# A two-block fp32 transformer kernel: joined seams, the compressed branch by token, and the convolution's layer norm in columns

## The chip, the cores and the metric

The kernel runs on one core of a Trainium2 chip. The metric is device time in microseconds (us) from start to end of one execution. Inputs and outputs are fp32 in HBM. The core has TensorE (PE in the rows), VectorE (DVE), ScalarE (ACT), GpSimd (POOL), SyncE (SP), and DMA queues that SyncE and ScalarE feed.

## What is computed

512 tokens of width 1024 pass a first block (latent attention beside a depthwise convolution, a gated FFN, a gated per-layer embedding) and then a second block of two layers: a short convolution mixer and an MLP, then a sparse attention and an MLP. The parts that the change touches, from the reference:

```python
def hybrid_mixer(xn, ...):                       # first block
    ...
    attn = causal_mla_attention(q_nope, q_rope, k_nope, k_rope, v)
    c = causal_depthwise_conv(a * jax.nn.sigmoid(gate), conv_w, conv_b)
    c = jax.nn.silu(layer_norm(c, conv_ln_g, conv_ln_b))
    return jnp.concatenate([attn, c], axis=-1) @ w_o

def first_block(...):
        ...
        h = h + rms_norm(ffn, g_ffn_post[i])
        e = rms_norm(p[i] @ w_ple_proj[i], g_ple[i])
        h = h + jax.nn.sigmoid(h @ w_ple_gate[i]) * e

def nsa_attention(...):                          # second block, layer 2
        logit_c = jnp.einsum('bqghd,bngd->bqghn', qt, k_cmp) + bias_c[None]
        p_c = jax.nn.softmax(logit_c, axis=-1) * has_any[None, :, None, None, None]
        o_c = jnp.einsum('bqghn,bngd->bqghd', p_c, v_cmp)
        ...
        o = gt[..., 0:1] * o_c + gt[..., 1:2] * o_s + gt[..., 2:3] * o_w
```

With 512 tokens the selection keeps every block, so selected and window branches are two softmaxes over the same causal range. The compressed keys are 31 blocks of 32 tokens, each passed through a two-layer MLP with SiLU (`phi`). `gt` are sigmoid gates, 16 heads by 3. `bias_c` and the other biases come from a table of relative positions.

## The kernel before

**Layout and precision.** Activations lie as channels in partitions and tokens in columns: `h[:, c, :]` is chunk c of 8, 128 channels by 512 tokens. An fp32 product is made of rounded halves: x = XH + XL, w = WH + WL, and three matmuls (WH·XH, WH·XL, WL·XH, `three`, lines 399 to 403). HH and HL are a second pair of such halves.

**Weights.** There are 301 units of 128x1024, loaded by SyncE in one fixed order into a ring of four slots, `raw`. ScalarE makes WH (`upper`, line 891), GpSimd makes WL = raw − WH (line 370), and a projection of TensorE waits for `wlo` and then runs 24 matmuls of 512 columns to a unit (`project`, `by_token`). `upper(b.u + k)` casts on ScalarE all units up to k ahead of the one in use, each when its slot has been released (`used`).

**Order.** Nothing is scheduled: each engine has its program written out by hand, in which it runs strictly in order, and semaphores join them. PSUM has eight banks of 128x512: 0 to 3 take output tiles in turn (`tile_done`, `tile_free`), 4 to 7 serve norms, tables and attention. VectorE or ScalarE evicts a tile, and VectorE makes the low half of every activation.

**Norms.** Squares are made by ScalarE (line 913) and added up by VectorE (line 1424); `total` sums over partitions on TensorE (line 492), ScalarE takes the root (line 920), VectorE the reciprocal (line 1430), `spread` brings it back as a full tile (line 501).

**Start.** VectorE computes the rotary angles (`rope_table`, line 1491) between the input projection's tiles 0 to 1 and 2 to 3, whose eviction is `channels(2)`, line 1517.

**First attention.** After the convolution (line 513, 128x128 matmuls) come the low-rank expansions: four units for the queries, two for keys and values. Then the layer norm's sum over channels (`ln_total`, line 521: fp32 matmuls with a stationary matrix of ones), then four pairs of heads: scores (534, 539), logits on VectorE, exponentials on ScalarE (1049), transposes (550), copies (1057), values (568), whose result ScalarE evicts (1063). The layer norm's second sum (521 again), its root, reciprocal, products, SiLU (1088) and splits stand inside pairs 1 to 3. Then the output projection `w_o`.

**FFN's end.** TensorE sums the squares, `spread`; VectorE makes h + norm chunk by chunk (1698, 1700) and its low half (1793); ScalarE makes the high half. The gate projection (8 units, two rounds of 4) starts on the first chunks. After each round ScalarE takes the sigmoid (1212), VectorE multiplies and adds, and `lower_chunk` (1795, 1799) prepares the first MLP's input, the short convolution mixer's.

**Tables.** In the second block's mixer, after its group j = 1, TensorE makes 16x1680 biases (line 581, four matmuls), VectorE copies them (1829), and ScalarE issues two DMAs that repeat them in HBM (`ftab`, `tab`, lines 1239, 1241); they are read back as bias strips in the attention.

**Compressed branch.** `phi` is two projections of 96 matmuls of 160 columns each; a second layer (746, 751); query projection (8 units in two rounds of 4); gates by token (96 matmuls of 48 columns); logits by key (24 matmuls of 512 columns, KCH stationary) into banks 0 to 3; VectorE copies them and adds the bias (2022, 2026); 16 transposes (774) bring them to tokens; VectorE takes maximum, difference (2038, 2041), later sum, reciprocal and product (2047 to 2058); 16 transposes (786) bring them back.

**Second attention.** 16 pairs, each of two heads in one of the two branches: scores (805), logits (2068), exponentials (1364), normalising (2085), transposes (817), copies of them (1370, `pair_copy`), values (831, 840), and after every second pair the eviction `pair_out` (1376, 1378). Then the output projection: two projections of four units, and the last MLP.

Of the kernel before, what the change touches and what calls it, by code (L numbers as in the profile page):

```python
# [8 lines left out]
S, D, P = 512, 1024, 128  # L9
# [4 lines left out]
PH = 4  # L14
# [40 lines left out]
n1_done t1_done p1_g0 p1_rest v1_done v1_out at_hi at_lo ln_sum ln_xc ln_sq ln_var ln_std ln_inv ln_xn ln_act cv_hi cv_lo warm y_out y_tmp e_g ffn_t ffn_g ffn_gelu ffn_u hid_s hid_hi  # L55
hid_lo r_ok v_ok y_ok cu_t tab_done tab_out tab_st bc_in col_ok kv_ok kr_ok kr_pad kr_hi kr_lo silu_ok
cmp_done kc_hi kc_lo vc_ok gate_s gate_ok c_lg c_mx lt_ok c_exp c_sum c_inv c_mul c_tr c_pt krep_hi krep_lo
# [69 lines left out]
def build(nc, io):  # L127
# [3 lines left out]
    with ExitStack() as ctx:  # L131
# [75 lines left out]
        ohs, relb, tabs, bcs = cut(12304, 1680), cut(13984, H2), cut(5636, 1680), cut(9728, GR, S)  # L207
# [12 lines left out]
        qst, L, PCT, LT = cut(6144, TT, S), cut(12288, TT, S), cut(6144, GR, S), cut(6144, GR, S)  # L220
# [6 lines left out]
        NMX, SUM, INV, COL, RC = 16, 32, 48, 80, 84  # L227
# [34 lines left out]
        LOGITS2 = (4, 6, 8)  # L262
        NP1 = H1 // 2
# [53 lines left out]
        def _(sp):  # L317
# [27 lines left out]
            for hd in range(H2):  # L345
                if hd < 4:
                    sp.wait_ge(sems["kr_lo"], 2)
                    if hd == 3:
                        sp.wait_ge(sems["lt_ok"], GR)
# [45 lines left out]
        def _(pe):  # L395
# [121 lines left out]
            def ln_total(x, ready, done):  # L517

                for c in range(4):
                    ready(c)  # L520
                    last = nc.tensor.matmul(ps[:, 6, :], ones[:, :], x[:, c, :], start=c == 0, stop=c == 3)
                last.then_inc(sems[done], 1)
# [20 lines left out]
            def mla_transposes(n, r):  # L543
                j = 2 * n + r
                pe.wait_ge(sems["n1_done"], 4 * (j + 1))
# [27 lines left out]
            def tables():  # L573

                pe.wait_ge(sems["onehot_in"], 16)
                pe.wait_ge(sems["relb_in"], 16)
                for k in range(0, 1680, S):
                    if k >= 2 * S:
                        pe.wait_ge(*m["tab_out"].upto(k // S - 1))
                    w = min(S, 1680 - k)  # L580
                    nc.tensor.matmul(ps[0:H2, 4 + k // S % 2, 0:w], relb[0:33, 0:H2], ohs[0:33, k:k + w],
                                     start=True, stop=True).then_inc(*m["tab_done"].tick())
                m["tab_out"].next(4)
# [1677 lines left out]
```

## Time and profile before

| what | value |
|---|---|
| median of 3 runs | 2014.56 us (2013.85 to 2014.84) |
| profiled execution, whole | 2016.62 us |
| its span, first to last instruction | 2014.6 us |
| mean granted TensorE clock | 0.965 |
| TensorE busy | 1914.2 us, 95% |
| VectorE, ScalarE, GpSimd busy | 992.1, 763.7, 756.5 us |
| DMA | 177.53 MB, 88 GB/s over the span |

Durations are read from the one profiled execution. "Busy" of TensorE includes time at a lower clock. The granted clock is a share of 2.4 GHz: 0.50 is the level of 1.2 GHz. A profile names each instruction by engine, source line and operation, and for an engine's idle time the instruction that ended it.

### The profile page before, as it was taken

The numbers are of one execution on the slowest core, as the hardware profiler recorded it, in microseconds if no ns is written. First come the engines' busy times: TensorE is split into PE (matmuls) and PEld (weight loads), VectorE is DVE, ScalarE is ACT, GpSimd is POOL, SyncE is SP. The second block draws the span as 40 slices with busy tenths as digits, with TensorE's granted clock in tenths as the row PEclk, the third lists the DMA queues.
The fourth block names the chain that finished last, engine by engine and source line by source line (L and its number), as shares of the span: only waits on it lengthen the run. The fifth ranks groups of instructions, "written<-read, shape, count | busy, mean of one in ns | idle before, by whom it ended". The sixth has DMA issues, their size and how long they took to land.

```text
span 2014.6 us, 25069 instructions
## 1 busy us (share of the span) xinstructions
PE 1914.2 (95%) x9252; PEld 1556.7 (77%) x9252; DVE 992.1 (49%) x1635; ACT 763.7 (38%) x1297; POOL 756.5 (38%) x319
## 2 busy tenths in 40 slices
PE   7899898999999799999999999999788899999997
PEld 6786586888888677888888888888655588888886
DVE  6656368543445644235433345631677635334444
ACT  6676544222223341233222223322288733222221
POOL 4412133534443332444554444534100035444442
PEclk9999899999999899999999999988799999999999
DMA  5202122332333233973333322333010123332321
GB/s 183 69 37 63 31 84 65 116 92 86 112 96 92 63 91 82 168 178 107 90 108 95 101 85 88 111 94 110 6 33 27 48 76 103 101 96 83 100 89 62
DMA packets 52236, 177.53 MB, mean 88 GB/s; under 512 B 5527, under 2 KB 5911, under 8 KB 52152
## 3 DMA queue, kind: packets, MB, share of 16 engines
q1 hardware_dynamic: 47952, 166.22, 26.7%
q10 hardware_dynamic: 4200, 10.15, 3.4%
q8 instruction: 57, 0.93, 0.2%
q14 instruction: 27, 0.22, 0.0%
HBM read 166.88 MB, written 9.47 MB: 88 GB/s over the span
## 4 chain that ended last, share of the span: by engine, by line
PE 81%; issue 9%; DVE 6%; POOL 2%; ACT 2%; DMA 0%; ACTq 0%; DVEq 0%; POOLq 0%
PE ps L401 25%; PE ps L402 25%; PE ps L403 25%; POOL WL L370 2%; PE ps L513 2%; DVE arena L2085 1%; DVE arena L2068 1%; PE ps L840 1%; PE ps L817 1%; PE ps L805 1%; ACT arena L1364 1%; DVE arena L1491 0%; PE ps L831 0%; ACT arena L1370 0%; DMA ident<-in_ident 0%
## 5 line engine op out<-in xcount | busy, mean ns | idle before, releaser
L370 POOL TENSOR_TENSOR WL<-raw,WH 128x1024 fp32r<-128x1024 f32 x295 | 736.0, 2509 | 1202.2 <-ACT WH L891 1202.1
L401 PE MATMUL ps<-XH,WH 128*128 128x512 f32 (+1 forms) x1280 | 503.1, 393 | 33.0 <-DMA ident<-in_ident 10.6
L891 ACT ACTIVATE WH<-raw 128x1024 fp32r<-128x1024 f32 x295 | 303.8, 1053 | 538.8 <-PE ps L403 481.5
L402 PE MATMUL ps<-XL,WH 128*128 128x512 f32 (+1 forms) x1280 | 500.9, 391 | 0.0
L403 PE MATMUL ps<-XH,WL 128*128 128x512 f32 (+1 forms) x1280 | 500.4, 391 | 0.0
L401 PE MATMUL ps<-HH,WH 128*128 128x512 f32 x1072 | 420.4, 392 | 3.7 <-DVE HL L1799 3.7
L402 PE MATMUL ps<-HL,WH 128*128 128x512 f32 x1072 | 419.0, 391 | 0.0
L403 PE MATMUL ps<-HH,WL 128*128 128x512 f32 x1072 | 418.8, 391 | 0.0
L401 PEld LDWEIGHTS ps<-XH,WH 128*128 128x128 f32 x1280 | 248.2, 194 | 85.4 <-issue 29.8
L403 PEld LDWEIGHTS ps<-XH,WL 128*128 128x128 f32 x1280 | 248.2, 194 | 49.1
L402 PEld LDWEIGHTS ps<-XL,WH 128*128 128x128 f32 x1280 | 248.2, 194 | 47.7
L401 PEld LDWEIGHTS ps<-HH,WH 128*128 128x128 f32 x1072 | 202.5, 189 | 46.2 <-issue 4.5
L403 PEld LDWEIGHTS ps<-HH,WL 128*128 128x128 f32 x1072 | 202.3, 189 | 42.5
L402 PEld LDWEIGHTS ps<-HL,WH 128*128 128x128 f32 x1072 | 202.3, 189 | 41.7
L1912 DVE TENSOR_TENSOR h<-h,ps 128x512 f32<-128x512 f32 x112 | 75.6, 684 | 161.0 <-PE ps L403 161.0
L1895 DVE SCALAR_TENSOR_TENSOR arena<-ps,rstd 128x512 f32<-128x512 f32 x64 | 44.0, 691 | 195.7 <-PE ps L403 188.7
L1447 DVE TENSOR_TENSOR XL<-arena,XH 128x512 fp32r<-128x512 f32 x88 | 129.9, 1516 | 14.9 <-ACT XH L1378 11.2
L1272 ACT ACTIVATE XH<-arena 128x512 fp32r<-128x512 f32 x64 | 40.4, 632 | 251.4 <-DVE arena L1895 251.4
L1364 ACT ACTIVATE arena<-arena,small 128x128 f32<-128x128 f32 (+3 forms) x128 | 70.5, 560 | 7.4 <-DVE small L2068 7.4
L2068 DVE CUSTOM_DVE_ANT_0 arena<-ps,arena 128x128 f32<-128x128 f32 (+3 forms) x128 | 56.1, 487 | 25.3 <-PE ps L805 23.4
L1424 DVE TENSOR_TENSOR acc<-acc,sq 128x512 f32<-128x512 f32 x70 | 57.8, 826 | 15.3 <-ACT sq L913 15.3
L1761 DVE TENSOR_TENSOR arena<-arena,ps 128x512 f32<-128x512 f32 x48 | 33.0, 687 | 65.4 <-PE ps L403 64.9
(236 smaller groups left out, 1730.3 us busy)
## 6 DMA issues: line engine op xcount, KB each, us to landing
raw<-in_weights SPq DMA_DIRECT2D x301, 512.0 KB, 3.6
tab<-arena ACTq DMA_DIRECT2D x1, 5120.0 KB, 78.6
arena<-tab SPq DMA_DIRECT2D x16, 256.0 KB, 3.6
ftab<-arena ACTq DMA_DIRECT2D x1, 2080.0 KB, 23.6
h<-in_xT SPq DMA_DIRECT2D x8, 256.0 KB, 8.7
out_T<-h SPq DMA_DIRECT2D x8, 256.0 KB, 2.1
arena<-ftab ACTq DMA_DIRECT2D x4, 256.0 KB
arena<-in_pT ACTq DMA_DIRECT2D x1, 512.0 KB, 3.5
```

What stands on the lines that cost most here:

```text
L370: nc.gpsimd.tensor_tensor(WL[:, s, :], raw[:, s, :], WH[:, s, :].bitcast(f32), SUB)\
L401: nc.tensor.matmul(out, wh, xh, start=start, stop=False)
L402: nc.tensor.matmul(out, wh, xl, start=False, stop=False)
L403: return nc.tensor.matmul(out, wl, xh, start=False, stop=stop)
L891: nc.scalar.activation(WH[:, s, :], raw[:, s, :], ACT.Copy).then_inc(*m["whi"].tick())
L1272: nc.scalar.activation(XH[:, 4 * par + 2 * pr + t, :], rt[:, 2 * pr + t, :], ACT.Square)\
L1364: nc.scalar.activation(a, a, ACT.Exp, bias=small[:, NMX + c:NMX + c + 1], scale=-1.0, accum_out=small[:, SUM + c:SUM + c + 1]).then_inc(se ...
L1424: V.tensor_tensor(acc[:, :], acc[:, :], sq[:, m["acc_add"].n % 2, :], ADD).then_inc(*m["acc_add"].tick())
L1447: V.tensor_tensor(out, src, up_.bitcast(f32), SUB).then_inc(*lo.tick())
L1895: V.scalar_tensor_tensor(rt[:, 2 * pr + t, :], bank(t), 0.0, rstd[:, :], MAX, MUL)\
L1912: V.tensor_tensor(h[:, c, :], h[:, c, :], bank(t), ADD).then_inc(*m["tile_free"].tick())
L2068: V.tensor_tensor_reduce(out=job.p(n, r)[:, POFF[qs]:POFF[qs] + w], in0=ps[:, 2 * (c % 2) + r, at:at + w], in1=strips[:, job.heads[r] % 4, ...
```

## The change

Eight parts, in the order of the program (names as in the code):

1. **Start**: `channels(2)` stands before `rope_table()` on VectorE.
2. **Layer norm of the convolution**: the sums are made in columns: `ln_columns` multiplies each 128x128 tile by a column of ones (32 fp32 matmuls with one column in all), the first after query unit 0, the second after unit 3; `ln_mean` spreads the mean with four transposes inside unit 1; root and reciprocal are taken on 128x4; products, SiLU and splits stand before the attention. Nothing of it is left inside but the four low halves on VectorE (n == 1), and `mla_values(0)` waits for nothing of it.
3. **FFN's end**: tables 0 and 1 are made before the sum of squares, 2 and 3 after `spread`; ScalarE copies them; their inputs are loaded in the FFN. The casts of the gate's units stand earlier on ScalarE.
4. **Gate to mixer**: chunks 0 to 3 are lowered after the gate's first round, 4 to 7 between the additions of the second.
5. **Mixer**: tables and their copies are gone from j = 1; ScalarE issues the two DMAs there as before.
6. **Compressed branch**: casts of `phi`'s second projection stand between the HH splits; the first round of queries stands before `phi`'s second layer; the bias goes into banks 4 to 7 by 16 fp32 matmuls (stationary bias, moving identity); the gates are one tile of 64 rows (24 matmuls of 512 columns, then four transposes, sigmoid from PSUM); logits are made by token on top of the bias (96 matmuls of 64 columns, stationary queries). Eight copies, four additions and 16 transposes go. VectorE's key splits stand among maximum and difference; pair 0's first scores, logits and exponentials stand before the softmax's end.
7. **Second attention**: `pair_out` is cut in two; the eviction stands before `pair_copy(n - 1, 1)`.
8. **Its end**: units 0 and 1 of `w_o2` stand around the last transposes.

The core of the diff:

```diff
-            for j in range(4):
-                project(1, 3, 2, HH, HL, m["qkv_lo"] if j == 0 else None)
+            project(1, 3, 2, HH, HL, m["qkv_lo"])
             m["qkv_lo"].next(3)
-            project(1, 2, 4, HH[:, 3:5, :], HL[:, 3:5, :], m["qkv_lo"])
+            ln_columns(cacc, convolved).then_inc(sems["ln_sum"], 1)
+            project(1, 3, 2, HH, HL, hooks={3: ln_mean})
+            project(1, 3, 2, HH, HL)
+            project(1, 3, 2, HH, HL)
+            ln_columns(lnsq, lambda c: pe.wait_ge(sems["ln_sq"], c + 1)).then_inc(*m["norm_sum"].tick())
+            project(1, 2, 4, HH[:, 3:5, :], HL[:, 3:5, :], m["qkv_lo"], hooks={4: spread})
...
             down(1, True)
+            pe.wait_ge(sems["onehot_in"], 16)
+            pe.wait_ge(sems["relb_in"], 16)
+            tables((0, 1))
             total(7, True)
             spread()
+            tables((2, 3))
...
-                if j == 1:
-                    tables()
...
+            project(4, 2, 4, HH, HL, m["x_lo"])
             for i in range(2):
                 pe.wait_ge(*m["silu_ok"].next(2))
...
+                    last = nc.tensor.matmul(ps[:, 4 + t, g * P:(g + 1) * P], bcs[:, g, t * P:(t + 1) * P], ident[:, :],
+                                            start=g == 0, stop=False, skip_group_check=True)
...
+            for c in range(DC):
+                w = slice(c * 3 * H2, c * 3 * H2 + 64)
+                last = three(ps[0:64, gates_bank, :], WH[:, s, w], WL[:, s, w], HH[:, c, :], HL[:, c, :], c == 0, c == DC - 1)
...
+                    for i, (q, key) in enumerate(((XH, KCH), (XH, KCL), (XL, KCH))):
+                        last = nc.tensor.matmul(ps[:, 4 + t, 64 * c:64 * c + 64], q[:, c, x], key[:, w],
+                                                start=False, stop=i == 2, skip_group_check=True)
...
+                if n == NP:
+                    pe.wait_ge(sems["l2_done"], 8 * NP)
+                    w_o2((0, 1))
                 if 1 <= n <= NP:
                     for r in range(2):
                         pair_transposes(n - 1, r)
+                if n == NP:
+                    w_o2((1, 2))
+            w_o2((2, 4))
...
             prepare()
+            channels(2)
             rope_table()
-            channels(2)
...
-            for j in range(3):
+            for j in range(2):
...
+                    if j and t:
+                        lower_chunk("norm_mix_0", c - 1)
...
+                if n >= 3 and n % 2 == 1:
+                    pair_evict((n - 3) // 2)
                 if 1 <= n <= NP:
                     pair_copy(n - 1, 1)
```

**Where instructions stand, at three places.** ScalarE at the FFN's end: casts (`WH<-raw`), squares (`sq`), root (`small<-ps`) and the high halves of h (`XH<-h`). Before, then after:

```order
L891 ACTIVATE WH<-raw 128x1024 [waits used,raw_in0]
L909 ACTIVATE acc<-arena 128x512 [waits norm_sum,tile_free]
L913 ACTIVATE sq<-arena 128x512 [waits acc_add,tile_free] x3
L891 ACTIVATE WH<-raw 128x1024 [waits used,raw_in1]
L913 ACTIVATE sq<-arena 128x512 [waits acc_add,tile_free] x4
L920 ACTIVATE small<-ps,small 128x4 [waits norm_sum]
L1198 ACTIVATE XH<-h 128x512 [waits h_upd]
L891 ACTIVATE WH<-raw 128x1024 [waits used,raw_in2]
L891 ACTIVATE WH<-raw 128x1024 [waits used,raw_in3]
L1198 ACTIVATE XH<-h 128x512 [waits h_upd] x7
L891 ACTIVATE WH<-raw 128x1024 [waits used,raw_in0]
```

```order
L922 ACTIVATE WH<-raw 128x1024 [waits used,raw_in0]
L940 ACTIVATE acc<-arena 128x512 [waits norm_sum,tile_free]
L944 ACTIVATE sq<-arena 128x512 [waits acc_add,tile_free] x3
L922 ACTIVATE WH<-raw 128x1024 [waits used,raw_in1]
L922 ACTIVATE WH<-raw 128x1024 [waits used,raw_in2]
L944 ACTIVATE sq<-arena 128x512 [waits acc_add,tile_free] x3
L922 ACTIVATE WH<-raw 128x1024 [waits used,raw_in3]
L944 ACTIVATE sq<-arena 128x512 [waits acc_add,tile_free]
L951 ACTIVATE small<-ps,small 128x4 [waits norm_sum]
L1229 ACTIVATE arena<-ps 16x512 [waits tab_done] x2
L1235 ACTIVATE XH<-h 128x512 [waits h_upd] x2
```

The cast of the unit that uses slot 2 has gone ahead of three of the squares, that of slot 3 ahead of the last one, and two copies of tables stand between the root and the first high half.

ScalarE at the compression: L1312 and L1347 split h for the queries, L1322 and L1361 are the SiLU of `phi`'s first projection. Before, then after:

```order
L1312 ACTIVATE HH<-h,vec 128x512 x8
L1322 ACT_TABLE_LOAD
L1322 ACTIVATE arena<-arena 128x128 [waits tile_free] x2
L891 ACTIVATE WH<-raw 128x1024 [waits used,raw_in0]
L891 ACTIVATE WH<-raw 128x1024 [waits used,raw_in1]
L891 ACTIVATE WH<-raw 128x1024 [waits used,raw_in2]
L891 ACTIVATE WH<-raw 128x1024 [waits used,raw_in3]
```

```order
L1347 ACTIVATE HH<-h,vec 128x512 x2
L922 ACTIVATE WH<-raw 128x1024 [waits used,raw_in0]
L1347 ACTIVATE HH<-h,vec 128x512 x2
L922 ACTIVATE WH<-raw 128x1024 [waits used,raw_in1]
L1347 ACTIVATE HH<-h,vec 128x512 x2
L922 ACTIVATE WH<-raw 128x1024 [waits used,raw_in2]
L1347 ACTIVATE HH<-h,vec 128x512 x2
L922 ACTIVATE WH<-raw 128x1024 [waits used,raw_in3]
L1361 ACT_TABLE_LOAD
L1361 ACTIVATE arena<-arena 128x128 [waits tile_free] x2
L922 ACTIVATE WH<-raw 128x1024 [waits used,raw_in0]
L922 ACTIVATE WH<-raw 128x1024 [waits used,raw_in1]
```

Four casts that stood behind the SiLU now stand among the splits, which wait for nothing.

TensorE from the logits of the compressed branch to the first scores of pair 0 (L805, after it L826). Before, then after:

```order
L401 MATMUL ps<-XH,KCH 64x512 [waits tile_free]
L402 MATMUL ps<-XL,KCH 64x512
L403 MATMUL ps<-XH,KCL 64x512
L774 MATMUL ps<-ident,arena 128x128 [waits lt_ok]
L774 MATMUL ps<-ident,arena 128x128 x15
L805 MATMUL ps<-HH,XH 128x128 [waits tile_free,krep_lo]
L805 MATMUL ps<-HH,XH 128x128
```

```order
L793 MATMUL ps<-KCL,XH 128x64
L793 MATMUL ps<-KCH,XL 128x64
L793 MATMUL ps<-KCH,XH 128x64
L793 MATMUL ps<-KCL,XH 128x64
L793 MATMUL ps<-KCH,XL 128x64
L826 MATMUL ps<-HH,XH 128x128 [waits gate_s,krep_lo]
L826 MATMUL ps<-HH,XH 128x128
```

Before, one matmul of 512 columns for a head pair's keys is the last and 16 transposes follow; now the last matmuls have 64 columns and the scores follow at once, waiting for gates and key splits.

## Rows read from the trace of the kernel before

**Rows 1.** the page: head, TensorE's busy time, shares of the chain

```profile
span 2014.6 us, 25069 instructions
...
PE 1914.2 (95%) x9252; PEld 1556.7 (77%) x9252; DVE 992.1 (49%) x1635; ACT 763.7 (38%) x1297; POOL 756.5 (38%) x319
...
PE 81%; issue 9%; DVE 6%; POOL 2%; ACT 2%; DMA 0%; ACTq 0%; DVEq 0%; POOLq 0%
```

**Rows 2.** TensorE's waits: line, releaser: us in total, times, longest

```profile
PE ps L831 <- ACT arena L1376: 9.6, 7, 2.6
PE ps L568 <- ACT arena L1063: 7.8, 2, 5.3
PE ps L401 <- DVE XL L1793: 7.5, 2, 3.8
PE ps L774 <- DVE arena L2026: 5.7, 1, 5.7
...
PE ps L786 <- DVE arena L2058: 5.5, 1, 5.5
PE ps L401 <- DVE arena L1517: 5.4, 1, 5.4
...
PE ps L401 <- issue: 4.3, 1, 4.3
...
PE ps L401 <- DVE HL L1799: 3.7, 1, 3.7
```

**Rows 3.** windows (us): length, busy us (instructions) by engine, TensorE's clock, DMA share, GB/s

```profile
171.10:239.90 68.80, 59.75 (x393) 38.70 (x392) 37.13 (x120) 46.29 (x112) 0.20 (x1) 0.90 0.03 9
...
725.30:729.30 4.00, 3.99 (x11) 3.15 (x12) 4.00 (x7) 3.79 (x7) 0.00 (x0) 0.57 0.00 2
793.80:800.30 6.50, 4.23 (x10) 0.74 (x9) 4.87 (x8) 1.23 (x2) 0.00 (x0) 0.77 0.00 0
800.30:804.20 3.90, 3.90 (x10) 3.11 (x10) 0.49 (x2) 0.00 (x0) 0.00 (x0) 0.51 0.61 65
1328.60:1342.20 13.60, 13.60 (x98) 13.35 (x96) 9.05 (x10) 8.60 (x12) 5.22 (x2) 1.00 0.26 77
...
1346.50:1367.00 20.50, 20.50 (x96) 20.50 (x97) 0.32 (x1) 1.00 (x2) 6.88 (x3) 0.50 0.33 103
1367.00:1371.80 4.80, 4.56 (x22) 4.27 (x22) 0.33 (x1) 4.18 (x5) 2.44 (x2) 0.50 0.00 0
...
1416.60:1421.90 5.30, 5.30 (x50) 5.30 (x48) 3.37 (x6) 2.09 (x3) 0.00 (x0) 1.00 0.01 2
1421.90:1432.00 10.10, 10.10 (x49) 10.10 (x50) 0.53 (x2) 0.00 (x0) 0.00 (x0) 0.50 0.01 2
...
1445.10:1469.70 24.60, 12.93 (x80) 10.03 (x80) 20.76 (x57) 10.65 (x31) 0.00 (x0) 0.71 0.04 11
1469.70:1594.10 124.40, 111.61 (x888) 71.77 (x888) 100.05 (x383) 108.23 (x331) 0.00 (x0) 0.99 0.15 43
...
1596.70:1603.00 6.30, 6.30 (x21) 1.96 (x21) 1.51 (x4) 0.61 (x1) 0.00 (x0) 0.51 0.01 3
```

**Rows 4.** the same columns, matmuls of line 513 alone

```profile
125.00:133.00 8.00, 8.00 (x74) 8.00 (x74) 1.00 0.01 2
```

**Rows 5.** timeline: start, us, TensorE's operation, count; one of two such rows

```profile
167.56 3.59 PE L521 MATMUL ps<-arena,ones 128*128 128x512 f32 x8
```

**Rows 6.** timeline of VectorE at the FFN's end

```profile
669.79 0.68 DVE L1793 TENSOR_TENSOR XL<-h,XH 128x512 fp32r<-128x512 f32 x1
...
673.17 2.83 DVE L1793 TENSOR_TENSOR XL<-h,XH 128x512 fp32r<-128x512 f32 x1
```

**Rows 7.** timeline of GpSimd in the same stretch

```profile
670.18 5.28 POOL L370 TENSOR_TENSOR WL<-raw,WH 128x1024 fp32r<-128x1024 f32 x2 [10.42 <-ACT WH L891]
```

**Rows 8.** timeline of ScalarE's queue at the tables

```profile
801.54 5.07 ACTq L1241 DMA_DIRECT2D tab<-arena  x1
```

**Rows 9.** timeline of GpSimd at the start

```profile
67.59 8.68 POOL L377 TENSOR_TENSOR WL<-raw,WH 128x512 fp32r<-128x512 f32 x6 [12.52 <-ACT WH L882]
```

More of the change, by code:

```diff
@@ L515, in conv_group, with ln_columns, ln_mean @@
                 last.then_inc(sems["tz_used"], 1)
-            def ln_total(x, ready, done):
+            def ln_columns(x, ready):
                 for c in range(4):
                     ready(c)
-                    last = nc.tensor.matmul(ps[:, 6, :], ones[:, :], x[:, c, :], start=c == 0, stop=c == 3)
-                last.then_inc(sems[done], 1)
+                    for t in range(TT):
+                        last = nc.tensor.matmul(ps[:, 7, t:t + 1], x[:, c, t * P:(t + 1) * P], ones[:, 0:1],
+                                                start=c == 0 and t == 0, stop=c == 3, skip_group_check=True)
+                return last
+            def ln_mean():
+                pe.wait_ge(sems["ln_mu"], 1)
+                for t in range(TT):
+                    last = nc.tensor.transpose(ps[:, 7, t * P:(t + 1) * P], small[:, MU + t:MU + t + 1].to_broadcast([P, P]),
+                                               ident[:, :])
+                last.then_inc(sems["ln_bc"], 1)
             def mla_scores(n, step):
@@ L571, in mla_values, with tables @@
                 last.then_inc(sems["v1_done"], 1)
[L573 to L581, printed above, removed]
+            def tables(part):
+                for i in part:
+                    if i == 3:
+                        pe.wait_ge(*m["tab_out"].next())
+                    w = min(S, 1680 - S * i)
+                    nc.tensor.matmul(ps[0:H2, 4 + i % 3, 0:w], relb[0:33, 0:H2], ohs[0:33, S * i:S * i + w],
                                      start=True, stop=True).then_inc(*m["tab_done"].tick())
-                m["tab_out"].next(4)
             pe.wait_ge(sems["const_ok"], 2)
@@ L1040, in _ @@
             close(1, 4)
+            for c in range(4):
+                act.wait_ge(sems["ln_xn"], c + 1)
+                nc.scalar.activation(cacc[:, c, :], cacc[:, c, :], ACT.Silu, bias=col("conv_ln_b", c),
+                                     scale=col("conv_ln_g", c)).then_inc(sems["ln_act"], 1)
+            act.wait_ge(sems["used"], b.u + 1)
+            for c in range(4):
+                act.wait_ge(sems["ln_act"], c + 1)
+                nc.scalar.activation(WOH[c], cacc[:, c, :], ACT.Copy).then_inc(sems["cv_hi"], 1)
             close(1, 4)
@@ L1595, in _ @@
             for j in range(4):
+                if j == 1:
+                    dve.wait_ge(sems["ln_sum"], 1)
+                    V.tensor_scalar(small[:, MU:MU + TT], ps[:, 7, 0:TT], -1.0 / CC, None, MUL).then_inc(sems["ln_mu"], 1)
+                if j == 2:
+                    dve.wait_ge(sems["ln_bc"], 1)
+                    for c in range(4):
+                        V.tensor_tensor(cacc[:, c, :], ps[:, 7, :], cacc[:, c, :], ADD).then_inc(sems["ln_xc"], 1)
                 if j % 2 == 0:
@@ L1618, in _ @@
             close(1, 4)
+            root_ = inverse(False)
+            for c in range(4):
+                V.tensor_tensor(cacc[:, c, :], cacc[:, c, :], root_, MUL).then_inc(sems["ln_xn"], 1)
             for t in range(4):
```

343 lines of the change are left out of this document (167 added, 176 removed).

## The prediction

> **What bounds the kernel now.** I read the page first: TensorE is busy 1914.2 of 2014.6 us and has 81% of the chain [rows 1]. So it is the bound, and only 100.4 us of idle time can be won, plus the stretches in which it is busy at half its clock. The waits of TensorE say where the idle time lies [rows 2], and windows over those places say at which clock it worked behind each wait [rows 3]: the reader should look at the count of matmuls, at the busy time, and at the clock's column (0.50 is 1.2 GHz, 1.00 is 2.4 GHz). A projection's matmul of 512 columns takes 0.227 us at full clock (10.9 us for 48; 0.39 at 0.51, as 10 in 3.90 us show [rows 3]); of narrow ones 50 take 5.3 us at full clock and 49 take 10.1 at half [rows 3], so 0.106 and 0.206 each. Small seams, each with a wait and a slow stretch behind it, make up what the change goes for. The profiled execution took 2016.62 us; the sum below is made against it, and the median of the runs stands 2.06 lower, so the same difference is taken from 2014.56.
>
> **1. Start: +0.9 us (0 to 5.4).** TensorE waits 5.4 for line 1517, which stands behind the rotary table on VectorE [rows 2]. Ahead of the table it takes the wait away. But GpSimd makes the halves of these weights at 8.68 for two units [rows 9], 4.3 each, while TensorE would use one in less, and its first lower (67.6) hangs on a cast that ScalarE does after the table's sine. The table and with it the sine end 1.2 later (two evictions stand ahead), so the first is ready at 73.2; TensorE, started 5.4 earlier at 57.8, has done its 48 matmuls (10.9) at 68.7 and waits 4.5. 5.4 − 4.5 = 0.9.
>
> **2. Layer norm: +6.5 (3 to 9).** Removed are two sums of 3.6 on TensorE, one ahead of the attention and one inside [rows 5], both waits for line 1063 (7.8), which ScalarE reaches late behind the SiLU, splits and table loads of the norm [rows 2], and part of a slow stretch: 68.8 us at clock 0.90 [rows 3]. Added ahead of the attention: 32 fp32 matmuls of one column, twice. No row shows a matmul so narrow. An fp32 matmul writes two records, and line 513's run 74 in 8.00 us [rows 4], 0.108 each, so 32 records are 3.5 at the most if width costs anything; I take 3.2 for each sum, 0.5 for each of two spreads, and 1.2 that the value copies of VectorE now stand behind four products. That is 8.6 less the sum of 3.6 removed: the scores start 5.0 later. Inside go 3.6 of the sum, 5.3 of the longer wait of line 1063, and 2.6 of slow matmuls (68.8 at 0.90 hold 6.9 of slow time in all, and I leave most of it); the shorter wait of 2.5 I leave. 3.6 + 5.3 + 2.6 − 5.0 = 6.5. If the clock keeps falling it is 3.9, if both waits go 9.
>
> **3. FFN's end: +0.6 (−1 to 4).** TensorE waits twice, 7.5 in all, for the low halves of line 1793 [rows 2]. The first took 0.68 and the third 2.83 [rows 6], with GpSimd in two weight units from 670.18 on, 5.28 long [rows 7]; VectorE's op ends when the lowers end. The casts now stand before the root, so this collision goes (3.5), but the same two lowers then lie beside the adding of squares, on the path to the norm: 3.0. The tables' four matmuls and ScalarE's copies lie in the waits for the root and for the first low halves. I take the difference, 0.6.
>
> The Trainium skill, page "SBUF — State Buffer", section "Who interferes with whom", has VectorE and GpSimd share a port pair that one instruction holds to its end; the two rows agree (2.83 beside GpSimd, 0.68 alone). By that rule the gain of the moved cast is given back by the place it moves to, as above; without it this seam would give some 4.
>
> **4. Gate to mixer: +5.2 (3.6 to 5.5).** The wait for line 1799 (3.7) ends because chunks 0 to 3 are ready since the first round and the rest follow one by one beside the second; behind it 11 matmuls took 3.99 at clock 0.57 [rows 2, 3], 1.5 more than at 0.227. 3.7 + 1.5 = 5.2.
>
> **5. Tables out of the mixer: +6.7 (3 to 8.1).** The window of 6.5 holds the four matmuls and their waits for the copies; it goes, and so do 1.6 of the 10 slow matmuls behind it (3.90 − 2.27) [rows 3]. New: ScalarE now issues the large DMA (5.07, with the other 5.9 [rows 8]) as soon as its splits are done (796.6 in the trace), still ahead of the cast for a unit that TensorE reaches near 804.7: the issue ends at 802.5, a cast takes 1.05 and a lower 2.5, so 806.1. It waits 1.4. 6.5 + 1.6 − 1.4 = 6.7.
>
> **6. Compressed branch: +25.3 (16 to 32).** From the end of `phi`'s first projection (1342.2) to the first transposes of pair 0 (1469.7) it takes 127.5 us now. After:
> - the second projection: 96 matmuls of 160 columns. Before, an "issue" wait of 4.3 (casts behind the SiLU) and then 20.5 at clock 0.50 [rows 2, 3]. The casts now come earlier; at full clock, as the first projection ran (96 in 13.6 [rows 3]), it ends at 1355.7. This is the largest single gain, 11.3.
> - first queries 96 × 0.227 = 21.8, to 1377.4; `phi`'s second layer 2.3 at full clock (half of the 4.8 at 0.50 [rows 3]), 1379.7; second queries, 1401.5.
> - bias: 16 fp32 matmuls, 32 records at the 0.108 to 0.113 of line 513 [rows 4]: 3.6, 1405.1.
> - gates: 24 × 0.227 = 5.4 in place of 96 narrow ones (5.3 + 10.1 [rows 3]): 1410.6.
> - logits: 96 of 64 columns. The gates' 48 columns fell to half clock after 50, so I take 47 × 0.111 + 49 × 0.206, and 0.6 for the gate's transposes: 15.9, 1426.5. All at full clock would be 1421.8.
> - then VectorE, in the durations that the same instructions have in the window of 24.6, where it is busy 20.76 in 57 [rows 3]: last maximum 0.7 and difference 0.6, pair 0's first logits 2.1, `has_any` 0.2, four sums 2.5, reciprocal 0.6, products 0.4 + 2.5, the next logits 1.3 and 1.1, exponentials behind the copies and two casts 2.0, inverse and normalising 1.5, and 2.4 for collisions with the two lowers and gaps between the steps: 17.9, 1444.4.
>
> So 1469.7 − 1444.4 = 25.3; in it are the waits of 5.7 and 5.5 for lines 2026 and 2058 [rows 2], which go or fall into the 17.9. Low end: second projection still slow (−7) and a longer chain; high end: full clock in the logits (+5).
>
> **7. Second attention: +7.8 (−4 to 9).** TensorE's values wait 9.6 in seven places for ScalarE's eviction of line 1376 [rows 2], which is queued behind three copies. Moved ahead of them it comes 1.1 us earlier each time: 7.8. The rival is in the same line: the copies start 0.6 later, and if the transposed tiles are what TensorE lacks, 7 × 0.6 = 4 are lost. I take the gain, since the waits name 1376 and none names the copies.
>
> **8. Its end: +2.4 (1 to 5).** The longest of the seven waits, 2.6 [rows 2], stands ahead of the last transposes and is filled by unit 0: 1.5 beside the 1.1 already counted. Behind it 21 transposes and values took 6.3 at clock 0.51 [rows 3], where full clock would save some 3; I take 0.9 of it.
>
> **Sum.** 0.9 + 6.5 + 0.6 + 5.2 + 6.7 + 25.3 + 7.8 + 2.4 = 55.4; 2016.62 − 55.4 = 1961.2, and by the median 2014.56 − 55.4 = **1959.2**. All low ends together (21.6) give 1993, all high ends (78) 1937.
>
> **Rivals.**
> - *The clock stays low in narrow work.* `phi`'s second projection runs at 0.50 although nothing stops it long, and the logits fall as soon as the gates did: 7 from the projection, 4 from logits and gates, 1 from the start of the queries: 55.4 − 12 = 43, 1971. For it: 0.50 has held through 96 busy matmuls once [rows 3]. Against: the first projection, of the same form, ran at 1.00.
> - *Waits move to the weights.* In seams 1, 3, 5 and 6 ScalarE's casts and GpSimd's lowers come last; with 3 us each not counted above, 1971. For it: two of the four already show that releaser in my own sum.
> - *More than forecast:* full clock through the logits (+5), no collisions (+4.5), no wait at the tables' issue (+1.4): 1948.
> - *Part 2 does not do what it says:* the norm costs its 5.0 ahead of the attention, and VectorE and ScalarE, busy 37.1 and 46.3 of 68.8 [rows 3], set the pace inside, so the wait of line 1063 only changes its name: 55.4 − 11.5 = 44, 1970.5.
> - *Slower.* One mechanism: the clock falls in the 96 logits, as it did in the gates, and does not come back in the attention. TensorE is busy 111.6 of 124.4 us there in seven double pairs [rows 3], 15.9 of 17.8 each; at half clock 31.9, 14.1 more each. The other parts give 55.4 − 7.8 = 47.6, so from the fourth double pair on the kernel is slower, and with all seven it is at 2014.6 + 99 − 47.6 = 2066. Against: the clock was 0.71 in the 24.6 us ahead of the attention and 0.99 in it. The Trainium skill, page "TensorE: Matmul & The Clock Gate", section "Part 4: PE-mode transpose", says that transposes do not keep the clock up as matmuls do, which speaks for it; the trace does not agree, since the window with all the attention's transposes stands at 0.99.
>
> **How the numbers follow.** Forecast 0.5 (1951 to 1968); low clock 0.17; weights 0.12; more than forecast 0.09; part 2 fails 0.07; slower 0.03; and 0.02 for many small failures at once, half of which end within 0.2% (4 us, about what a measurement of this kernel can tell from no change) and half just below it. So faster 0.96, same 0.01, slower 0.03. The range of 8 in 10, **1942 to 1980**, reaches above to two rivals together and below a little past the better case.
>
> **What would show it.** In the profile after: no wait for line 1793's or 1799's successors above 1 us; no wait after `phi`'s first projection, its second in 13.5 us at clock 1.00; the 96 logits in 11 to 16 us; pair 0's transposes about 102 us behind `phi`'s first projection; the wait for the eviction shorter than 2 us in total, the double pair 16.2 instead of 17.3 to 17.8; the start's wait renamed to GpSimd's line. It would be wrong if the clock's column shows 0.50 in the second attention, if a new ScalarE or VectorE wait of several us stands before pair 0, or if the double pair keeps its length.

## The result, and the profile after

The changed kernel takes 1967.84 us (median of 4 runs, 1965.12 to 1970.67) against 2014.7 before: a ratio of 0.9767, 95% interval 0.975 to 0.9784, so 46.9 us faster. The forecast was 1959.2. The profiled execution took 1970.67 us, 45.95 less than the one of before. Its page, against [rows 1]:

```profile
span 1968.7 us, 25202 instructions
...
PE 1904.0 (97%) x9328; PEld 1556.1 (79%) x9328; DVE 981.5 (50%) x1617; ACT 760.4 (39%) x1298; POOL 757.8 (38%) x319
...
PE 82%; issue 9%; DVE 5%; POOL 2%; ACT 1%; DMA 0%; ACTq 0%; DVEq 0%; POOLq 0%
```

TensorE is idle for 64.7 us instead of 100.4 and busy 10.2 less. Its waits (line, releaser: us in total, times, longest), against [rows 2]:

```profile
PE ps L838 <- DVE arena L2127: 7.5, 8, 2.8
PE ps L493 <- DVE acc L1481: 5.9, 3, 3.8
PE ps L808 <- DVE arena L2114: 5.6, 1, 5.6
PE ps L402 <- POOL WL L371: 5.4, 3, 3.2
PE ps L402 <- POOL WL L378: 4.3, 1, 4.3
...
PE ps L579 <- ACT arena L1107: 2.5, 1, 2.5
PE ps L402 <- DVE XL L1851: 1.6, 2, 1.3
...
PE ps L852 <- ACT arena L1428: 1.3, 1, 1.3
...
PE ps L402 <- DVE HL L1857: 0.8, 2, 0.5
```

The waits for lines 1517, 1376 (now 1428), 2026, 1829 and the "issue" wait are gone or nearly so. New at the start is the wait for GpSimd's line 378, 4.3. The wait for VectorE's normalising (now line 2127) has grown from 5.6 in nine to 7.5 in eight, 2.8 of it ahead of pair 0's transposes. Windows of the changed kernel, in the columns of [rows 3] (length, then TensorE, its weight loads, VectorE, ScalarE and GpSimd with busy us and instructions, then TensorE's clock, DMA share and GB/s); they are cut at TensorE's own steps:

```profile
143.54:147.23 3.69, 3.69 (x34) 3.69 (x32) 1.38 (x2) 0.63 (x1) 0.00 (x0) 0.94 0.02 4
147.23:150.77 3.54, 3.54 (x11) 2.78 (x12) 0.76 (x2) 0.00 (x0) 0.00 (x0) 0.58 0.00 0
161.43:165.96 4.53, 4.53 (x34) 4.53 (x33) 1.29 (x2) 4.30 (x7) 2.92 (x2) 0.77 0.35 100
165.96:170.99 5.03, 5.03 (x14) 3.91 (x14) 0.87 (x2) 0.86 (x2) 3.59 (x2) 0.53 0.44 123
180.61:237.45 56.84, 53.22 (x384) 36.45 (x384) 29.25 (x111) 36.21 (x100) 4.73 (x2) 0.97 0.07 20
658.09:674.61 16.52, 10.49 (x32) 5.75 (x31) 11.25 (x15) 5.77 (x11) 5.06 (x2) 0.62 0.31 95
...
770.10:830.30 60.20, 60.20 (x267) 49.87 (x266) 22.85 (x31) 12.83 (x14) 24.17 (x10) 1.00 0.71 130
1314.17:1341.03 26.86, 26.86 (x194) 26.86 (x193) 18.14 (x12) 16.80 (x21) 21.66 (x9) 1.00 0.44 134
...
1395.98:1414.18 18.20, 18.20 (x102) 18.03 (x101) 10.20 (x15) 10.00 (x15) 2.36 (x1) 0.60 0.01 1
1414.18:1433.62 19.44, 9.97 (x66) 7.98 (x65) 15.68 (x46) 11.12 (x31) 4.74 (x2) 0.68 0.00 0
1433.62:1443.40 9.78, 9.64 (x64) 6.29 (x65) 8.03 (x33) 8.17 (x26) 0.00 (x0) 0.83 0.17 54
1433.62:1551.93 118.31, 111.32 (x888) 71.80 (x888) 100.56 (x388) 108.66 (x333) 0.00 (x0) 0.99 0.14 46
```

From places in TensorE's order that both programs have, stage by stage (the two profiled executions):

| stage | forecast | gained |
|---|---|---|
| 1 start, to the convolution's end (140.25 / 139.36) | 0.9 | 0.9 |
| 2 layer norm, to the attention's last values (239.93 / 237.45) | 6.5 | 1.6 |
| FFN, unchanged code (660.24 / 658.09) | 0 | −0.3 |
| 3 FFN's end and gate (721.66 / 719.75) | 0.6 | −0.2 |
| 4 gate to mixer (741.93 / 736.00) | 5.2 | 4.0 |
| 5 tables out of the mixer (1328.60 / 1314.17) | 6.7 | 8.5 |
| 6 compressed branch (1469.73 / 1433.62) | 25.3 | 21.7 |
| 7 second attention (1596.70 / 1551.93) | 7.8 | 8.7 |
| 8 its end (1651.70 / 1605.69) | 2.4 | 1.2 |
| sum | 55.4 | 46.1 |

So 8.5 of the 9.3 us that are missing lie in parts 2 and 6. In part 2 the two sums of 16 column matmuls (two records each) take 3.69 and 4.53 instead of 3.2, and what stands behind each runs at 0.58 and 0.53 of the clock. In part 6 the 96 logits take 18.20 at 0.60, and the chain behind them 19.44 at 0.68.

### The profile page after: what moved, and what is told of

The parts are those of the page before. It is cut to its first block, busy times and chain, and to the rows that moved or that the text cites. A ratio compares the mean times of both kernels' runs of the same rounds, so it can differ in the third digit from the quotient of the medians.

```text
span 1968.7 us, 25202 instructions
## 1 busy us (share of the span) xinstructions
PE 1904.0 (97%) x9328; PEld 1556.1 (79%) x9328; DVE 981.5 (50%) x1617; ACT 760.4 (39%) x1298; POOL 757.8 (38%) x319
## 4 chain that ended last, share of the span: by engine, by line
PE 82%; issue 9%; DVE 5%; POOL 2%; ACT 1%; DMA 0%; ACTq 0%; DVEq 0%; POOLq 0%
PE ps L402 25%; PE ps L403 25%; PE ps L404 25%; POOL WL L371 2%; PE ps L838 2%; DVE arena L2127 1%; PE ps L826 1%; PE ps L861 1%; PE ps L514 1%; DVE arena L2088 1%; PE ps L793 1%; ACT arena L1042 1%; DVE arena L1548 0%; PE ps L493 0%; DMA ident<-in_ident 0%
## 5 line engine op out<-in xcount | busy, mean ns | idle before, releaser
L402 PE MATMUL ps<-HH,WH 128*128 128x512 f32 (+1 forms) x1080 | 423.9, 393 | 0.8 <-DVE HL L1857 0.8
L403 PE MATMUL ps<-HL,WH 128*128 128x512 f32 (+1 forms) x1080 | 421.6, 390 | 0.0
L404 PE MATMUL ps<-HH,WL 128*128 128x512 f32 (+1 forms) x1080 | 421.6, 390 | 0.0
L402 PEld LDWEIGHTS ps<-XH,WH 128*128 128x128 f32 x1280 | 244.1, 191 | 75.6 <-issue 18.0
L404 PEld LDWEIGHTS ps<-XH,WL 128*128 128x128 f32 x1280 | 244.1, 191 | 48.7
L402 PEld LDWEIGHTS ps<-HH,WH 128*128 128x128 f32 (+1 forms) x1080 | 203.4, 188 | 43.7 <-DVE HL L1857 1.6
L404 PEld LDWEIGHTS ps<-HH,WL 128*128 128x128 f32 (+1 forms) x1080 | 203.2, 188 | 43.1
L403 PEld LDWEIGHTS ps<-HL,WH 128*128 128x128 f32 (+1 forms) x1080 | 203.4, 188 | 42.2
```

What stands on the lines that cost most here:

```text
L402: nc.tensor.matmul(out, wh, xh, start=start, stop=False)
L403: nc.tensor.matmul(out, wh, xl, start=False, stop=False)
L404: return nc.tensor.matmul(out, wl, xh, start=False, stop=stop)
```

## The experiments

Each kernel is the changed one with one edit, unless said otherwise. The diffs are abridged; `...` stands for lines left out. Windows are read from the one profiled execution of each. Their times are compared by the ratio to the kernel before, run beside them; the changed kernel's is 0.9767.

**Part 2 taken back** (sums of 512 columns, the second inside the attention, as in the kernel before).

> The changed kernel with part 2 alone taken back (the convolution's layer norm as before: sums by 512-column matmuls, the second and all that follows inside the attention). The trace of the changed kernel has 41.2 us from the end of the convolution to the first attention scores (30.8 before) and 56.8 in the attention (68.8 before), so part 2 gave only about 1.5. If these stages tell the whole story: 30.8 and 68.8 return, and the kernel is 1 to 2 us slower than the changed one (about 1969.5, ratio to the kernel before 0.9775). If part 2 was worth the 6.5 that I forecast and something else took 5 us: 1974.

1971.36 us, ratio 0.9779 (0.9763 to 0.9796). Before the scores, then in the attention to its last values:

```profile
138.97:169.82 30.85, 30.85 (x131) 23.93 (x129) 13.71 (x20) 13.93 (x21) 14.08 (x6) 1.00 0.29 86
169.82:238.40 68.58, 59.49 (x391) 38.68 (x392) 37.13 (x120) 46.30 (x112) 0.21 (x1) 0.90 0.03 9
```

30.85 and 68.58 against 41.25 (139.36 to 180.61) and 56.84: 10.4 more ahead, 11.7 less inside, and no more than 1.5 for the whole. The two intervals overlap, so the whole time alone does not tell the kernels apart. The attention did give what I had expected of it (11.5); the price ahead of it was twice the one that I had put (5.0).

**The mean's sum by four 512-column matmuls.**

```diff
-            ln_columns(cacc, convolved).then_inc(sems["ln_sum"], 1)
-            project(1, 3, 2, HH, HL, hooks={3: ln_mean})
+            ln_wide(cacc, convolved).then_inc(sems["ln_sum"], 1)   # ones stationary, all tokens moving
+            project(1, 3, 2, HH, HL)
```

> The changed kernel with the first of the layer norm's sums made by four fp32 matmuls of 512 columns at the same place (no mean's transposes, VectorE subtracts straight from the full tile). Theory 1, an unbroken run of one-column matmuls makes the clock fall: the sum takes 3.6 instead of 3.7, and the 9 matmuls behind it run at full clock (2.1 instead of 3.5), so the stretch from convolution to scores shrinks from 41.2 by about 1.9. Theory 2, the clock falls there whatever stands there (for instance by what the convolution did before): the 9 matmuls behind stay at 3.5, and only 0.4 is gained. In both the second, one-column sum still takes 4.5 and has 12 slow matmuls behind it (5.0).

```profile
143.06:146.09 3.03, 3.03 (x9) 1.35 (x8) 2.08 (x3) 0.63 (x1) 0.00 (x0) 1.00 0.00 0
146.09:149.90 3.81, 3.81 (x17) 2.99 (x16) 0.45 (x1) 0.60 (x1) 0.00 (x0) 1.00 0.00 0
138.85:177.95 39.10, 38.27 (x167) 30.44 (x166) 18.14 (x29) 19.35 (x31) 9.45 (x4) 0.91 0.19 54
```

The sum takes 3.03 at full clock, what follows stays at 1.00 (17 matmuls in 3.81; the changed kernel needed 3.54 for 11), and the stretch is 39.10: 2.1 less, theory 1. The edit takes out the mean's four transposes too (0.35 in the changed kernel), so not all of the 2.1 is the clock. 1966.88 us, ratio 0.9761 (0.9744 to 0.9777): in the whole time, 2 us are less than the runs scatter.

**The column sums in pieces between wide matmuls.**

```diff
-            ln_columns(cacc, convolved).then_inc(sems["ln_sum"], 1)
-            project(1, 3, 2, HH, HL, hooks={3: ln_mean})
-            project(1, 3, 2, HH, HL)
-            project(1, 3, 2, HH, HL)
-            ln_columns(lnsq, ...)
+            project(1, 3, 2, HH, HL, hooks={c + 1: ln_column(cacc, ..., c, ...) for c in range(4)})
+            project(1, 3, 2, HH, HL, hooks={1: ln_mean})
+            project(1, 3, 2, HH, HL, hooks={c + 2: ln_column(lnsq, ..., c, ...) for c in range(4)})
```

> The changed kernel with both column sums cut into four pieces of four fp32 matmuls that stand between the 512-column matmuls of query units 1 and 3. Theory 1: no unbroken run, so the clock stays; each sum costs 3.2 and nothing behind it is slow, the stretch shrinks from 41.2 by 4.5 to 5 if no new wait for the squares appears (up to 1 us). Theory 2 (one-column matmuls lower the clock however they stand, since TensorE does little in them): the units around them run at half clock in part, and the stretch is 41 or longer.

```profile
139.28:151.90 12.62, 12.62 (x75) 10.94 (x73) 3.44 (x6) 4.13 (x10) 0.00 (x0) 1.00 0.00 1
159.59:169.38 9.79, 9.79 (x42) 8.93 (x42) 0.69 (x1) 2.10 (x4) 1.87 (x1) 0.55 0.18 54
...
139.28:184.78 45.50, 42.40 (x196) 35.60 (x195) 18.31 (x30) 19.39 (x32) 9.52 (x4) 0.85 0.16 47
```

The first sum bears theory 1 out: units 0 and 1, the sum and three matmuls of unit 2 take 12.62 at clock 1.00. Its four pieces take 0.81 each from their start to the next matmul, 3.2 in all: the prediction's term is what the sum costs at full clock. The second doesn't: it begins with a wait of 2.3 for ScalarE's squares, and from there the mixture runs at 0.55. The stretch is 45.50, 4.3 longer. 1976.91 us, ratio 0.9812 (0.9795 to 0.9828), slower, though the profiled one of its runs took only 1971.25; where the other runs lose more stays open. Mixing held the clock here where nothing waited, and not behind a wait; and it ties every piece to its data.

**Bias and half of the logits between the second queries' matmuls.**

```diff
-            project(4, 2, 4, HH, HL)
+            hooks = {12 + t: lambda t=t: bias(t) for t in range(TT)}
+            hooks.update({... early(t, half) ...})        # 6 logit matmuls of 64 columns each, chunks 0 to 3
+            project(4, 2, 4, HH, HL, hooks=hooks)
...
-                for c in range(DC):                # the logits behind the gates
+                for c in range(4, DC):
```

> The changed kernel with the bias matmuls and half of the compressed logits (chunks 0 to 3, 48 matmuls of 64 columns in groups of 6) between the 512-column matmuls of the second query round; the other 48 stay behind the gates. In the changed kernel 96 of them took 18.2 (28 at 0.11, the rest at 0.21). Theory 1, the clock falls only after a long unbroken run of narrow matmuls: the 48 in groups cost 0.11 each (5.4), of the 48 behind some 28 run at full clock: 3.1 + 20 x 0.21 = 7.3; 18.2 - 12.7 = 5.5 us gained, and 1 more for a faster clock in the first scores. Theory 2, narrow matmuls lower the clock wherever they stand: gain 0 to 2, with slow 512-column matmuls among the groups.

Windows (four groups of six between wide matmuls; from the last logits to pair 0's transposes; pairs 0 and 1) and the one wait behind the logits:

```profile
1380.63:1392.84 12.21, 12.21 (x76) 10.80 (x75) 1.76 (x3) 1.26 (x2) 1.04 (x1) 1.00 0.01 1
...
1406.75:1429.54 22.79, 9.28 (x66) 7.50 (x65) 20.11 (x52) 14.52 (x36) 7.15 (x3) 0.65 0.00 0
1429.54:1443.59 14.05, 13.91 (x65) 8.31 (x65) 8.98 (x35) 8.47 (x26) 0.00 (x0) 0.56 0.12 37
```

```profile
PE ps L821 <- DVE arena L2127: 9.4, 1, 9.4
```

On TensorE theory 1 holds: the groups run at 1.00, and from the second projection's end to the last logits it takes 67.4 instead of 73.15: 5.7 less, where 5.5 was forecast. But VectorE, which makes the key splits in the same time, is not ready sooner: the wait for its products grows from 5.6 to 9.4, so pair 0's transposes come only 2.4 sooner. And the first two pairs take 14.05 at clock 0.56, where the changed kernel took 9.78 at 0.83. 1967.58 us, ratio 0.9764 (0.9746 to 0.9781): no gain. A faster TensorE lengthened a wait, which took back 3.3 of the 5.7. That the longer wait also cost the clock is not shown: between it and pair 0 the clock had come back (0.92 from 1421.98 to 1429.54), and directly ahead of pair 0's transposes TensorE waits 3.10 here and 2.81 in the changed kernel. Why it stays low for longer here is open.

**Another order behind the logits.** Pair 0's last scores and logits ahead of the compressed transposes and sums, its normalising ahead of pair 1's logits, and two weight casts earlier.

```diff
-                if n == 0:
-                    compressed_transposes()
                 if n < NP:
                     pair_scores(n, 2)
+                if n == 0:
+                    compressed_transposes()
...
                 nc.scalar.activation(L[:, t, :], L[:, t, :], ACT.Exp).then_inc(*m["c_exp"].tick())
+                if t in (1, 2):
+                    upper(b.u + 2 + t)
```

> The changed kernel with another order behind the compressed logits: pair 0's last scores stand before the compressed transposes, its last logits before the softmax's sums, its first normalising before pair 1's first logits, and the two weight casts that ScalarE did after the compressed copies stand between the exponentials of the compressed softmax. Theory 1, VectorE's chain sets the time from the last logits (1414.2) to pair 0's transposes (1433.6, so 19.4): the chain loses a wait for TensorE (3.2 in front of the last logits) and the collision with GpSimd in the normalising (3.56 for four operations that take 1.52 otherwise), and the transposes start 15 to 16 behind the last logits: 3.5 to 4.5 us gained, about 1964. Theory 2, TensorE at half clock sets it (the transposes and scores behind the 5.6 wait): less than 1.5 gained.

The window from the last logits to pair 0's transposes, and VectorE's four normalisings, here and then in the changed kernel, where GpSimd lowers two units beside them (from 1427.7, 4.74 long):

```profile
1412.53:1430.27 17.74, 11.10 (x66) 8.72 (x65) 14.53 (x50) 9.41 (x30) 0.44 (x1) 0.56 0.00 0
```

```profile
1424.59 1.52 DVE L2131 TENSOR_SCALAR arena<-arena,small 128x128 f32<-128x128 f32 x4
```

```profile
1429.91 3.56 DVE L2127 TENSOR_SCALAR arena<-arena,small 128x128 f32<-128x128 f32 x4
```

17.74 instead of 19.44, and 3.56 becomes 1.52 with the casts moved. By pair 0's first values it is 2.8 us, because the transposes ahead of them take 3.1 here and 4.2 there: between the two theories. VectorE's chain is part of it; but VectorE now waits 2.0 for pair 1's scores, which TensorE makes at half clock. 1967.05 us, ratio 0.9753 (0.9733 to 0.9772), an interval that overlaps the changed kernel's.

**Part 7 taken back.**

```diff
-                if n >= 3 and n % 2 == 1:
-                    pair_evict((n - 3) // 2)
                 if 1 <= n <= NP:
                     pair_copy(n - 1, 1)
+                if n >= 3 and n % 2 == 1:
+                    pair_evict((n - 3) // 2)
```

> The changed kernel with part 7 alone taken back: the eviction of a pair's output stands behind the copies again. If the wait for the eviction was the whole reason: the double pair goes from 16.11 back to 17.34 and the attention is 7 x 1.23 = 8.6 us longer, near 1976.5. If the copies were what counted, less than 3.

```profile
PE ps L852 <- ACT arena L1428: 9.5, 7, 2.6
```

The wait of [rows 2] is back to within a tenth of a microsecond, the double pair is 17.33 again (16.11 in the changed kernel), and the time is 1977.06 us, ratio 0.9813 (0.9793 to 0.9832). Two lines in another order are worth 9 us, and the copies, which start later for it, cost nothing.

**The compression's casts back behind the SiLU.**

```diff
-                        if c % 2:
-                            upper(b.u + 5 + c // 2)
-                else:
-                    upper(b.u + 7)
```

> The changed kernel with the casts of the compression's second projection put back behind the SiLU. Theory 1, the wait of 4.3 is what made the clock fall for the whole second projection: wait and 0.50 return, 26.9 for both projections becomes 38.4, and what follows starts at half clock too (3.6 more): 11.5 to 15 us slower, 1979 to 1983. Theory 2, the clock fell for another reason (what lies before has changed too): only the 4.3 return, 1972.

```profile
1331.63:1352.37 20.74, 20.73 (x96) 20.52 (x96) 0.32 (x1) 1.03 (x2) 6.89 (x3) 0.50 0.33 101
1357.07:1361.50 4.43, 4.43 (x11) 3.46 (x12) 0.00 (x0) 0.20 (x1) 4.43 (x3) 0.50 0.61 169
```

```profile
PE ps L402 <- issue: 9.0, 2, 4.7
```

The wait ahead of the second projection is back (4.3), the same 96 matmuls take 20.74 at 0.50 again, and because the next casts stand behind a SiLU as well, a second wait (4.7) and some ten more slow matmuls follow. 1986.33 us, ratio 0.9859 (0.9839 to 0.9878): 18.5 us for four casts' place, more than the 15 that I had expected at most.

**The gate's casts at their old place, and behind the fifth high half.**

```diff
-                upper(b.u + 3 + j)
+                upper(b.u + 3)
...
             for c in range(DC):
+                if c == 1:                      # second kernel: c == 5
+                    upper(b.u + 4)
```

> The changed kernel with the casts of the gate projection at their old place (one ahead of the squares, two behind the first high half of h). Theory 1 (my term of part 3): the collision of VectorE and GpSimd only moved, so the adding of squares gets its 3.8 wait back down to 1 or less and the waits for the low halves return (3.6 and 3.8); from the FFN's last matmul to the gate's second group it is 16.5 in the changed kernel and 15.8 in the one before: within 1 us of the changed kernel. Theory 2: the early casts are what let the gate start at once, and without them it is 3 us or more slower.

> The changed kernel with the gate's casts neither at the old nor at the new place: one ahead of the squares as in the kernel before, and the two that stood behind the first high half of h behind the fifth. If it is the two lowers' neighbourhood alone that costs (3.8 in the adding of squares in the changed kernel, 3.8 in chunk 1's low half in the one before), both waits go: from the FFN's last matmul to the gate's second group 12.1 to 12.6 instead of 16.5 (15.9 with the old place), 4 us faster. If the units are then late instead: a wait of 2 or more for the lower appears some 11 us into the gate, and less than 2 is gained.

In the changed kernel VectorE's adding of squares and, later, the low half of h stand thus, and GpSimd beside the first:

```profile
658.76 2.25 DVE L1481 TENSOR_TENSOR acc<-acc,sq 128x512 f32<-128x512 f32 x1
660.93 0.68 DVE L1819 TENSOR_TENSOR arena<-arena,ps 128x512 f32<-128x512 f32 x1
661.53 2.24 DVE L1481 TENSOR_TENSOR acc<-acc,sq 128x512 f32<-128x512 f32 x1
...
671.89 0.69 DVE L1851 TENSOR_TENSOR XL<-h,XH 128x512 fp32r<-128x512 f32 x1
```

```profile
655.14 8.07 POOL L371 TENSOR_TENSOR WL<-raw,WH 128x1024 fp32r<-128x1024 f32 x3 [9.67 <-ACT WH L922]
```

The additions take 2.25 and 2.24 beside it, and the low half 0.69 after it. Line 1819, between the additions, reads one operand from PSUM and takes 0.68 in GpSimd's midst. The Trainium skill, page "SBUF — State Buffer", section "Who interferes with whom", says just this: an operation of VectorE with two SBUF inputs contends with a GpSimd operation that reads SBUF, and one with at most one SBUF input doesn't, unless it runs in a two-port mode. The trace agrees for these two lines. That a single SBUF tensor as input is no protection by itself shows in the normalising above (line 2127, 3.56 beside GpSimd for 1.52); no run here shows in which mode it ran.

From the FFN's last matmul to the gate's second group, casts at the old place and then late:

```profile
656.63:672.55 15.92, 9.34 (x32) 4.62 (x31) 11.64 (x15) 6.79 (x12) 5.28 (x2) 0.62 0.22 66
```

```profile
653.52:666.82 13.30, 10.26 (x32) 5.54 (x31) 8.11 (x15) 4.82 (x10) 0.00 (x0) 0.61 0.12 39
```

15.92 with the old place, 16.52 in the changed kernel, 13.30 late (12.1 to 12.6 expected); in this last one the last two additions (0.68 each) and the first four low halves (0.68 to 0.69) stand beside no lower. The collision is still there, with the fifth low half (2.90), but TensorE has four chunks of work before it. The gate's own 189 matmuls then take 44.50 instead of 45.14. 1967.26 us (ratio 0.9764, 0.9744 to 0.9783) with the old place and 1963.68 (0.975, 0.973 to 0.9769) late: what the late place gives is read from this window, for the intervals of the whole time overlap the changed kernel's.

**All that helped, in one kernel,** with a quarter of the logits mixed in, and the same without the mixing.

> All that the runs so far speak for: the wide sum for the mean (2.2), the new order behind the logits with the early weight casts (2.6), the late gate casts (4), and bias plus a quarter of the logits (24 matmuls of 64 columns) between the matmuls of the second query round (gates end 2.7 later, logits end 5.6 earlier against that, so 2.5 to 3 if VectorE's key splits do not bind). 1967.8 - 11 = 1956 to 1958.

> The same without the mixed logits: 1967.8 - 8.8 = 1959. If VectorE's chain, not TensorE's slow logits, sets the compressed branch, it is equal to the combined kernel within 1 us; if TensorE does, it is 2.5 to 3 slower.

1953.33 us, ratio 0.9696 (0.9673 to 0.9719), and 1953.53, ratio 0.9696 (0.968 to 0.9712). Both are 14 us faster than the changed kernel, more than the 11 and the 8.8 forecast; where the 3.3 and 5.5 us beyond them come from stays open. In the first, the last 72 logits, the chain, and pairs 0 and 1:

```profile
1389.66:1400.39 10.73, 10.73 (x77) 10.55 (x75) 9.86 (x15) 9.95 (x15) 2.46 (x1) 0.78 0.00 1
1400.39:1418.40 18.01, 11.07 (x65) 8.67 (x64) 15.86 (x51) 11.03 (x33) 4.77 (x2) 0.56 0.00 1
1418.40:1427.11 8.71, 8.15 (x67) 4.99 (x65) 7.24 (x31) 8.01 (x27) 0.00 (x0) 1.00 0.19 60
```

The logits now run at 0.78, and pairs 0 and 1 take 8.71 at 1.00 instead of 9.78 at 0.83. Whether the mixing itself gains anything, the two times don't tell: their runs reach from 1949.7 to 1957.8 and from 1951.5 to 1961.3. The traces tell it for this stage. From the end of `phi`'s second projection to pair 0's transposes, with the mixing and then without:

```profile
1331.81:1418.40 86.59, 79.65 (x434) 67.00 (x432) 37.49 (x85) 34.50 (x65) 26.09 (x11) 0.88 0.20 63
```

```profile
1336.59:1427.42 90.83, 84.39 (x434) 71.90 (x432) 36.55 (x85) 34.76 (x65) 25.95 (x11) 0.83 0.20 60
```

In these two executions the mixing gives 4.2 there, which speaks for TensorE's slow logits, and against VectorE's chain alone, as what sets this stage.

## Why the prediction was right, and where it was not

- **Part 1**, right to its wait: 4.3 for line 378, as in the term (4.5).
- **Part 2**: the step "I take 3.2 for each sum" failed, and so did its bound, "3.5 at the most", which came from a row at full clock; and a term behind it was missing. (It is 16 matmuls of one column twice, 32 records each, as the sum has it, and not 32 twice.) The sums took 3.7 and 4.5, and the clock fell in them, which cost 1.5 and 2.3 in the next 9 and 12 matmuls (3.54 and 5.03 instead of 2.04 and 2.72). I had asked what these matmuls cost and not what they leave to those behind. The price ahead was 10.4 instead of 5.0 (3.7 + 4.5 + 0.7 for two spreads + 1.5 + 2.3 + a wait of 0.8 for the value copies, less the old sum's 3.5, make 10.0 of it); the gain inside, 12.0 by the stages, was right.
- **Part 3**: right in mechanism. The collision went (0.69 for the low half) and came back in the additions (2.25 and 2.24), and both old and new place cost about the same. What I did not see is the third place, behind the fifth high half, where the stretch is 3.2 shorter. (The slow low half of [rows 6] is the second, not the third, and the slot 2 cast went ahead of four squares, not three; no term rests on either.)
- **Part 4**: 4.0 instead of 5.2; waits of 0.8 in all for line 1857 remain, at clock 1.00 (0.4 is unexplained).
- **Part 5**: the step "ScalarE now issues the large DMA (5.07)" failed, to the good. The issue took 0.63, and the casts followed at once:

```profile
790.77 0.63 ACTq L1276 DMA_DIRECT2D tab<-arena  x1
791.51 3.04 ACT L922 ACTIVATE WH<-raw 128x1024 fp32r<-128x1024 f32 x3 [0.83 <-issue]
```

  It took 0.63 in all twelve kernels profiled after the change and 5.07 only in the kernel before, so this is no scatter; why it took 5.07 there was not tried and stays open.
- **Part 6**: the second projection gave 11.6 (11.3 forecast) and ran at 1.00. The logits fell to half clock after 28, not 47: 18.2 instead of 15.9. The chain took 19.4 instead of 17.9; the collision that I had put in it is there (3.56 for 1.52), but TensorE's own steps at 0.68 lengthen it too: VectorE waits 3.2 for pair 0's last scores. What the rest of part 6 gave (10.1: gates in one tile, logits by token, fewer copies and transposes) is read from the stage, and no run takes it back by itself.
- **Parts 7 and 8**: the evictions gave 1.23 each where 1.1 was forecast; the end 1.2 instead of 2.4. Parts 1, 4, 5 and 8 were not taken back either; for them the stages and the waits that are gone speak.
- **Rivals**: of "the clock stays low in narrow work" the part on the logits came true by half (18.2, where all of them at half clock would be some 20.4 and the forecast was 15.9), and the same happened in part 2, where the rival had not looked; the second projection, its largest piece, ran at 1.00. "Waits move to the weights" came only at the start, where the sum had it: the other waits for GpSimd's halves are 5.4 in three, 5.3 before. "Part 2 does not do what it says" named the right part with the wrong mechanism: the gain inside came, and the price ahead took it. "Slower" did not come: the attention ran at 0.99 for 118.31 us, although it began at 0.83.
- **The total** came nearer than its parts: of the nine rows of the table, parts 5 and 7 gave 2.7 more than forecast, against 12.0 missing in the others.
- **The signs**: the double pair (16.11), the second projection (1.00) and the wait for the eviction (1.3) came as said. The 96 logits (18.2) did not, nor pair 0's transposes, 106 us behind `phi`'s first projection instead of 102; and the wait of 2.8 for VectorE ahead of pair 0 (0.7 before) comes near one that the prediction had listed against itself.

## What to carry to other kernels

A moved cast, eviction or copy is worth what waits behind it, and the largest gains here (18.5 and 9 us) are changes of order of a few lines. Price a step on TensorE with what it leaves behind: here runs of one-column matmuls cost another 1.5 and 2.3 in the wide ones behind them, and a wait of 4.3 was followed by 96 matmuls at half clock. A faster step on one engine can also do no more than lengthen its next wait for another. Where two engines disturb each other, look for the place where neither is on the path, before moving the collision from one seam to the next.

## What the runs showed of the hardware

Sixteen fp32 matmuls of one column took 3.69 and 4.53 us in one run each, and the 9 and 12 wide ones behind them ran at a mean granted clock of 0.58 and 0.53; in four pieces between wide ones they took 3.2 at 1.00. Four fp32 matmuls of 512 columns do the same sum in 3.03 at 2.4 GHz and leave the clock up. Without a gap, 192 matmuls of 160 columns ran at 1.00, and of 96 with 64 columns the last 68 or so at half clock. The issue of the same 5120 KB DMA took 5.07 in one place and 0.63 in another.
